# The first three modulation chunks summed on TensorE, x requested first, and token-side sums in a new order in a hybrid decoder layer

## What is computed

```
c_act = silu(c)
mod = c_act @ w_ada + b_ada                  # w_ada is 1024 x 9216: nine chunks of 1024 columns
(sh1, sc1, gt1, sh2, sc2, gt2, sh3, sc3, gt3) = split(mod, 9)
u = rmsnorm(h, ffn1_norm) * (1 + sc1) + sh1
h = h + 0.5 * gt1 * ((silu(u @ W_gate) * (u @ W_up)) @ W_out)     # d_ff 2816
u = rmsnorm(h, mix_norm) * (1 + sc2) + sh2
h = h + gt2 * token_mixer(u)
u = rmsnorm(h, ffn2_norm) * (1 + sc3) + sh3
h = h + 0.5 * gt3 * ffn(u)
out = rmsnorm(h, final_norm)
```

## Time and profile before

| | us |
|---|---|
| median of 3 runs (2450.9 to 2457.41) | 2453.93 |
| the profiled execution, its own time | 2455.61 |
| its span, first to last instruction | 2453.8 |
| TensorE busy in it | 2265.0 (92%) |
| GpSimd busy in it | 1419.5 (58%) |
| VectorE busy in it | 1210.2 (49%) |

### The profile page before, as it was taken

The page is one execution under the profiler, slowest core; times in us unless marked ns, Lnnn a source line. Parts: engine busy times, 40 slices in busy tenths (PEclk is TensorE's granted clock), DMA queues, the critical chain, the costliest instruction groups (busy, mean ns, idle before and its releaser), DMA issues.

```text
span 2453.8 us, 29962 instructions
## 1 busy us (share of the span) xinstructions
PE 2265.0 (92%) x10497; PEld 1832.8 (75%) x10497; DVE 1210.2 (49%) x2043; ACT 535.2 (22%) x1003; POOL 1419.5 (58%) x1294
## 2 busy tenths in 40 slices
PE   3679999999999899989998899999699999999997
PEld 3467777777888687767777788888478888888886
DVE  4955666565444714756555511141834444444444
ACT  4401101000111522444554401021411111111114
POOL 8757776777777633231122133335777777777774
PEclk6789999999999899999999999999899999999999
DMA  7143333332111311000011013111011111111112
GB/s 250 33 117 116 95 103 98 115 112 58 53 52 55 108 52 35 2 27 18 27 35 35 26 43 120 43 52 35 26 43 52 51 51 51 51 51 51 51 51 78
DMA packets 174358, 154.83 MB, mean 63 GB/s; under 512 B 5439, under 2 KB 149954, under 8 KB 174018
## 3 DMA queue, kind: packets, MB, share of 16 engines
q1 hardware_dynamic: 174274, 153.71, 20.7%
HBM read 145.30 MB, written 8.39 MB: 63 GB/s over the span
## 4 chain that ended last, share of the span: by engine, by line
PE 71%; DVE 9%; POOL 7%; issue 5%; ACT 4%; DMA 3%; SPq 0%; POOLq 0%; DVEq 0%; ACTq 0%
PE ps L1992 25%; PE ps L2042 20%; PE ps L1956 11%; PE ps L1909 11%; DMA ada_half<-in_w_ada 2%; POOL w_hi L810 1%; DVE h L1704 1%; POOL bufs L823 1%; DVE h L1727 1%; ACT rar L1086 1%; POOL w_lo L812 1%; DMA w_raw<-in_ffn_w_in 1%; ACT h L1222 1%; DVE rar L1580 1%; PE ps L2170 1%
## 5 line engine op out<-in xcount | busy, mean ns | idle before, releaser
L2042 PE MATMUL ps<-hid,w_hi 128*128 128x512 f32 x1408 | 446.9, 399 | 26.7 <-DVE mod L1387 24.0
L812 POOL TENSOR_TENSOR w_lo<-w_raw,w_hi 128x512 fp32r<-128x512 f32 x328 | 442.8, 1350 | 27.4
L810 POOL TENSOR_SCALAR w_hi<-w_raw 128x512 fp32r<-128x512 f32 x328 | 233.6, 712 | 301.9 <-PE ps L2042 178.1
L1992 PE MATMUL ps<-t,w_hi 128*128 128x512 f32 x1280 | 396.9, 391 | 0.0
L1526 DVE SCALAR_TENSOR_TENSOR h<-ps,gate_c,h 128x512 f32<-128x512 f32 x352 | 264.1, 751 | 209.1 <-PE ps L2042 209.1
L781 POOL TENSOR_SCALAR w_hi<-w_raw 128x1024 fp32r<-128x1024 f32 x57 | 61.0, 1070 | 517.2 <-PE ps L1909 324.1
L2042 PEld LDWEIGHTS ps<-hid,w_hi 128*128 128x128 f32 x1408 | 269.0, 192 | 89.2 <-POOL w_lo L812 19.4
L2042 PE MATMUL ps<-hid,w_lo 128*128 128x512 f32 x704 | 279.4, 397 | 0.0
L1992 PEld LDWEIGHTS ps<-t,w_hi 128*128 128x128 f32 x1280 | 240.5, 188 | 51.5
L1992 PE MATMUL ps<-t,w_lo 128*128 128x512 f32 x640 | 250.8, 392 | 0.0
L1992 PE MATMUL ps<-b_low,w_hi 128*128 128x512 f32 x640 | 201.4, 396 | 14.7 <-DVE bufs L1472 13.5
(11 more groups left out here) (242 smaller groups left out, 3912.2 us busy)
## 6 DMA issues: line engine op xcount, KB each, us to landing
w_raw<-in_ffn_w_in SPq DMA_DIRECT2D x88, 512.0 KB, 3.9
ada_half<-in_w_ada SPq DMA_DIRECT2D x112, 256.0 KB, 2.7
w_raw<-in_ffn_w_out SPq DMA_DIRECT2D x44, 512.0 KB, 3.6
w_raw<-in_w_in SPq DMA_DIRECT2D x41, 512.0 KB, 3.8
ada_full<-in_w_ada SPq DMA_DIRECT2D x16, 512.0 KB, 8.6
x_tile<-in_x SPq DMA_DIRECT2D x8, 512.0 KB, 4.8
h_dram<-h SPq DMA_DIRECT2D x1, 4096.0 KB, 12.0
h<-h_dram SPq DMA_DIRECT2D x1, 4096.0 KB, 13.4
```

Of the source, the lines that this page charges most:

```text
L810: nc.gpsimd.tensor_scalar(hi, src, 1.0, 0.0, ALU.mult, ALU.add).then_inc(hs_high, 1)
L812: nc.gpsimd.tensor_tensor(lo, src, hi.bitcast(F32), ALU.subtract).then_inc(hs_ready, 1)
L1992: mm = nc.tensor.matmul(ps[bank][:], w[i], x[:, k, :], start=(first and k == 0 and q == 0), stop=(k == 3 and q == 2), skip_group_check=True)
L2042: mm = nc.tensor.matmul(ps[4 + i % 4][:], w[:, r // 2, c], x[:, j, half(hf)], start=(j == 0 and q == 0), stop=(j == 1 and q == 2))
```

## The change

- **Chunks 0, 1 and 2 on TensorE.** `chunk_piece(m, k)` multiplies row block k of the chunk, as eight 128 x 128 weights, with column k of `c_act` (one column) and accumulates over k in PSUM: 64 products for a chunk in place of eight VectorE instructions and eight products. Chunks 0 and 1 stand in the opening of TensorE, chunk 0 ahead of the first `mean_square` and chunk 1 ahead of the second. The pieces of chunk 2 stand in classic tile 0: one behind each k of set 1 from the third on, two behind set 2.
- **Loads.** All eight x tiles have a buffer each and are requested without a wait ahead of any of w_ada; `ada_full` lies elsewhere in SBUF, over T1's and T4's place. Chunks 1 and 2 are requested block by block as TensorE frees `ada_full`. The requests of chunk 2 stand ahead of unit 3's weights. Nothing of chunk 2 is left in `ada_half`.
- **The order behind the norm.** GpSimd splits unit 3 ahead of the token sums (it waits for set 3), and in the first feed-forward its token sums wait for all of chunk 2. VectorE takes `chunk_out(2)` and the gate ahead of its token sums. T2 comes ahead of T1, and high parts, low parts, SiLUs and hidden products of the classic tiles are interleaved. TensorE waits for `mod_ready` before set 7, which writes the bank of chunk 2's sums.
- **The loop.** `chunk_out` of chunks 3 to 8 moves to the third step of the fast tile; in group 1 there are no column sums and no wait before `down`.

TensorE in the opening, before: the transposes, the partition sums of the squares (`bufs`), the column sums (`ada_acc`), then set 1 (`b_low`).

The core of the diff:

```diff
-            x_tile = [at(st_, f"x_tile{j}", [P, D])[:] for j in range(3)]
-            ada_full = at(st_, "ada_full", [P, KT, D])
-            ada_acc01 = [at(st_, f"ada_acc{j}", [P, D])[:] for j in range(2)]
+            x_tile = [at(st_, f"x_tile{j}", [P, D])[:] for j in range(TT)]
...
+            at(st_, "pad_ada", [P, (FRONT + 96 * 1024) // 4])
+            ada_full = at(st_, "ada_full", [P, KT, D])
...
+            def chunk_piece(m, k):
+
+                pe.wait_ge(ada_in[k], 16 * (m + 1))
+                for j in range(KT):
+                    mm = nc.tensor.matmul(sum_cols(m)[:, j:j + 1], ada_full[:, k, tile(j)], c_act[:, k:k + 1],
+                                          start=(k == 0 and j == 0), stop=(k == KT - 1), skip_group_check=True)
+                mm.then_inc(ada_used, 1)
...
+            pe.wait_ge(c_ready, 1)
+            for k in range(KT):
+                chunk_piece(0, k)
             mean_square(0, 0)
-            column_sums(0)
+            for k in range(KT):
+                chunk_piece(1, k)
             mean_square(0, 1)
-            column_sums(1)
             ffn(0)
...
+                        if f == 0 and (t, hf, i) == (1, 0, 0):
+                            pe.wait_ge(mod_ready, 3)
...
+                            if f == 0 and (t, hf, i) == (0, 0, 0) and k >= 2:
+                                chunk_piece(2, k - 2)
+                        if f == 0 and (t, hf, i) == (0, 0, 1):
+                            chunk_piece(2, KT - 2)
+                            chunk_piece(2, KT - 1)
...
             for t in range(TT):
-                if t >= 3:
-                    sp.wait_ge(x_t, 2 * (t - 3) + 2)
-                sp.dma_start(x_tile[t % 3], a["x"][0][t * P:(t + 1) * P, :]).then_inc(x_in[t % 3], 16)
-                if t == 2:
-                    for k in range(KT):
-                        ada_whole(0, k)
+                sp.dma_start(x_tile[t], a["x"][0][t * P:(t + 1) * P, :]).then_inc(x_in[t], 16)
...
+                if f == 0:
+                    for k in range(KT):
+                        ada_whole(2, k)
                 up_col(f, 0, 1, H + 2)
...
+                classic_unit(f, 3)
+                if f == 0:
+                    pool.wait_ge(ada_used, 3 * KT)
                 token_sums(f)
-                classic_unit(f, 3)
...
                 nc.vector.tensor_tensor(g1_b, u3_b, ps[2][:], ALU.add).then_inc(tile_step, 1)
+                if m is not None:
+                    chunk_out(m)
                 piece_of()
...
-                    fast_tile(f, 2 * g, b, piece_of)
-                    if sums:
-                        chunk_out(g + 1)
-                        dve.wait_ge(mod_ready, g + 2)
...
+                    fast_tile(f, 2 * g, b, piece_of, g + 1 if sums else None)
                     residual(f, g - 1, False, piece_of)
```

More of the change, by code:

```diff
@@ L236, in build_program @@
         c_ready = sem("c_ready")
-        x_in = [sem(f"x_in{j}") for j in range(3)]
+        x_in = [sem(f"x_in{j}") for j in range(TT)]
         x_t = sem("x_t")
@@ L689, in _ @@
                         sp.dma_start(vec[r0:r1, :], src.rearrange("(r c) -> r c", c=P)).then_inc(vec_in, 16)
-            for k in range(KT):
-                ada_whole(1, k)
+            for m in range(2):
+                for k in range(KT):
+                    ada_whole(m, k)
             ffn(0)
@@ L877, in token_sums @@
                     nc.gpsimd.tensor_tensor(t4_raw[:, i], u10, u11, ALU.subtract).then_inc(t_pool, 1)
-                for what in ("T1", "T2", "T3"):
+                for what in ("T2", "T1", "T3"):
                     for i in (1, 3):
@@ L1070, in ffn @@
             def ffn(f):
-                for what in ("T1", "T2", "T3"):
-                    for i in range(4):
-                        t_high(f, what, i)
                 classic(f)
@@ L1453, in token_sums, with t_lows @@
                                                    ALU.subtract).then_inc(t_dve, 1)
-                for what in ("T1", "T2", "T3"):
-                    for i in (0, 2):
-                        t_low(q, what, i)
+            def t_lows(q, what):
+                for i in (0, 2):
+                    t_low(q, what, i)
             def low(f, t, jj, hf):
@@ L1531, in ffn @@
             def ffn(f):
+                if f == 0:
+                    chunk_out(2)
+                    dve.wait_ge(mod_ready, 3)
+                    nc.vector.tensor_scalar(gate_c[:, 0, :], mod[:, 2 * KT:3 * KT], 0.5, None,
+                                            ALU.mult).then_inc(gate_ready, 1)
+                    dve.wait_ge(gate_ready, 1)
                 token_sums(f)
@@ L2079, in add_columns @@
                     def add_columns():
-                        if not (isinstance(g, int) and g == 1):
-                            pe.wait_ge(acc_done, DOWN * (f * GROUPS + g - 1))
+                        pe.wait_ge(acc_done, DOWN * (f * GROUPS + g - 1))
                         column_sums(g + 1)
```

131 lines of the change are left out of this document (57 added, 74 removed).

## The result

The changed kernel takes 2415.15 us (median of four runs, 2411.93 to 2419.01), where the kernel before takes 2455.49 (four runs, 2450.9 to 2457.41). The ratio is 0.9839, with a 95% interval of 0.9817 to 0.9861. That is 40 us faster; forecast were 37.

A forecast was written before the change was run, and what follows sets the result against it. TensorE, busy 2265.0 of 2453.8 us, was taken to bound the kernel. The terms summed as +6 (opening to first `down`) - 32 - 11 = -37, from 2453.9 to 2417 us; range 2374 to 2434, some 85%.

The forecast's parts named there:

- Term A: Opening up to the norm: one-column products mostly at clock 0.50 start the norm at 72.9 us, not 59.9; +13 us.
- First rival: Opening and set 1: clock stays high through the one-column products, norm at 51.2 us, total 2380 us; chance 16%.
- Term B: Norm to first `down`: GpSimd's queue sets it, 107.1 us instead of 114.1; -7 us, or +6 together with the opening.
- Term C: Groups 2 to 7: the wait ahead of `down` and the half clock behind it go; -32 us.
- second rival: Groups' loop: the wait ahead of `down` turns into one ahead of the column sums; total 2440 us; chance 8%.
- Term D: Second feed-forward, same new order without chunk 2: `down` starts 51.8 us behind unit 3's split, at 1810.1; -11 us.
- Third rival: One-column pieces: accumulation in PSUM makes each cost 5.1 us or more instead of 3.41; 2464 us at 2.2 more; chance 4%.

The follow-up runs named there:

- row_open: Changed kernel with operands of chunks 0 and 1 swapped: c's column as weights, w_ada block moving, two 512-column products a block; 2400.86 us, ratio 0.9764.
- pool_twice: Changed kernel with GpSimd computing each of its two low parts of T1 four times instead of once, in both feed-forwards; 2433.89 us, ratio 0.9899.
- undo_d: Changed kernel with the second feed-forward in the old order on GpSimd, VectorE and ScalarE; 2429.06 us, ratio 0.9911.
- undo_c: Changed kernel with the chunk's bias add put back behind the fast tile's seventh step in groups 2 to 7; 2451.37 us, ratio 0.9989.
- only_c: Kernel before with only the chunk's bias add moved ahead of the fast tile's fourth step in groups 2 to 7; 2418.63 us, ratio 0.9862.
- vec_open: Changed kernel with chunks 0 and 1 back on VectorE and column sums, in the new order of loads; 2400.75 us, ratio 0.9784.

## Why the prediction was right, point by point

**Term A (+13).** Measured +12.4: the norm starts at 72.28, forecast 72.9. The mechanism held: transposes ended at 18.2 (19), a block costs 3.41 us at 0.50, chunk 1 takes 27.31 (27.3). Three smaller terms were off and cancelled, which is luck. The stream began 1.0 us earlier than in my sum. The value I chose to lie between two bounds, 5 us at the high clock behind the transposes, was some 3 us (1.00 from 18 to 20 us, and 0.50 in all of 22 to 40), so that chunk 0 took 24.8 us instead of 23.1. And from the last column to the norm it was 0.4 us instead of 1.75: the small instruction for the scale takes 0.17 us now and took 1.47 before, while GpSimd was splitting weights. The Trainium skill (TensorE: Matmul & The Clock Gate, Part 4: PE-mode transpose) says that transposes do not bring the full clock. The changed kernel does not decide that, since its clock was 1.00 already at 6 us; it only shows 1.00 through the transposes and the fall behind them. The kernel before does: there the clock was 0.50 up to 25 us and 1.00 from 26 us on, with nothing but the 24 transposes begun at 21.54 in between, so the measurement goes the other way.

**First rival (the clock stays up).** It fell, and row_open shows what it missed: a TensorE that is busy without a gap is at 0.50 with products of one column and at 1.00 with products of 512. The Trainium skill (same page, Part 1: The HAM clock gate, What's actually happening) has keeping TensorE busy lift the clock; by that rule both kernels should have been at 1.00. A high clock at their start does not save it: the two blocks from 112.95 on run at 1.00 to their end, and behind them, with TensorE busy all the time, it is 0.58 from 116 to 118 us (0.83 in the window from 110 to 120).

**Term B (-7).** Measured in this profile: 178.24 - 72.28 = 106.0, so -8.1. GpSimd is the releaser of `down`, as forecast, and pool_twice shows that its queue sets the stretch. But parts of the sum were off and cancelled. The token sums took 10.7 us and not 13.5, since VectorE had done its own by then (117 to 123). That was the reason I gave for a lower bound of -14, which it does not yield: eight instructions at 0.4 us less are 3.2 us, so -10. Instead GpSimd waits 1.67 us, while ScalarE makes the high parts in the new order. From the first token sum to `down` it was 50.7 us where I had 51.8. TensorE alone is at `down` 105 us behind the norm and not 98, since it waits 3.44 us for VectorE ahead of the fast tile and then starts it at the half clock; of the margin of 9 us that my sum gave it, 0.92 were there.

Unit 3 was split 51.7 us behind the norm where I had 51.4, and that is luck twice. Within this profile set 1 and 2 were 1.5 us shorter than in my sum and set 3, which I had at the high clock, was 7.4 us and not 5.5, because the clock falls behind the two blocks ahead of it. And other profiles with the same instructions up to there have 56.2 (undo_d: 127.01 - 70.84), 56.1 (undo_c) and 55.7 (pool_twice). Two of the six blocks in set 1 run faster in the one (81.78: 2.03 us), all six take 3.41 us in the others. With undo_c and undo_d (norm at 70.9, first `down` at 181.3) A is +11, B -3.6, and A+B +7.4; with the 171.40 of only_c for the kernel before it would be +10. So +6 is right within a spread of some 5 us, and B = -7 alone rests on one profile.

**Term C (-32).** Measured -32.4. Both ways of the prediction come to it, the wait plus the half clock as well as the length of a group without a wait: column sums are 62.7 us apart (231.6 to 544.9 in five groups; forecast 62.3). undo_c and only_c show it alone, in both directions. The second rival, that the wait turns into one for VectorE's pieces, did not come: TensorE has no wait ahead of the column sums.

**Term D (-11).** Measured -9.6. The forecast of 51.8 us behind unit 3 is 1779.83 - 1726.90 = 52.9. In this feed-forward both engines do their token sums together, so 1.7 us an instruction was right here. The path on TensorE was not in the sum: it waits 9.17 us for VectorE ahead of the fast tile and is at `down` only 0.69 us before GpSimd's weights.

**Third rival (accumulation makes the product dearer).** It did not come: 3.41 us a block, to the hundredth what `column_sums` costs at that clock. No run shows its 5.1 us.

**The remainder.** The sum was -37, the medians say -40, this pair of profiles -44. Of the 5.9 us in stretches that the change does not touch, the windows show some as clock (700 to 826 us before at 0.99, the same work, 672 to 798 us, now at 1.00; the first units of the mixer 0.98, now 1.00). undo_c (3.0 us behind group 7) and undo_d (2.0 us) have longer spans in such places as well. I take it for the spread between executions, which was not tested further: four runs of the changed kernel lie some 7 us apart.

## What to carry over

A wait that is short in itself, but long enough for TensorE's clock to fall, costs about one and a half times its length (32.7 us for waits of 22.3): look at the granted clock behind a wait before pricing it, and look first for a small instruction that stands at the end of another engine's queue for no reason. When a reduction is put on TensorE, let the large operand move and the vector stand as weights: the same work then ran at twice the pace, because the clock stayed up. When a queue is shown to set a stretch, look how far behind it the next path is: here TensorE was less than 1 us away. And when two kernels differ by several edits, price each alone; here one bias add, moved forward, was nearly the whole gain, and two larger edits paid each other off.

## What the hardware showed that I had not expected

- Products of one column in 4-byte floats leave the granted clock at 0.50 with TensorE busy for 27 us on end, and take it down from 1.00: 3.41 us for 128 x 1024 numbers. The same numbers as the moving operand take 1.74 us at 1.00.
- Which blocks of a mixed stretch (products of 512 columns between blocks of one-column products) run at the high clock differs from one execution to the next: 51.7 us from the norm to the split of unit 3 in one profile, 55.7 to 56.2 in three others with the same instructions up to there.
- VectorE and GpSimd slowed each other where both worked on large 4-byte operands, in the opening as in the token sums: 2.1 to 2.3 us for a VectorE step on 1024 columns (vec_open) against 1.37 (the kernel before, 12.55 to 22.2 us), and 2.1 us for a GpSimd add on 512 columns (vec_open) against 1.37 (the changed kernel); a token sum on GpSimd took 1.7 us against 1.3.
